# A complex recurrence rewritten as a real scan of turned drives, its matrices built on GpSimd, and the experts' last step shared between two engines

## The reference, cut to what matters

```python
act = gelu(einsum('td,ted->te', hx, expert_u[ix]))
out = einsum('te,ted->td', gx * act, expert_v[ix])
```

```python
# x_t = Lbar x_{t-1} + Bbar u_t ; y_t = Re(C x_t) + D u_t      (Lbar, Bbar, x, C complex)
lb_re, lb_im = mag * cos(li * step), mag * sin(li * step)
_, _, x_re, x_im = lax.associative_scan(_complex_combine, (a_re, a_im, bu_re, bu_im), axis=1)
y = einsum('gcp,blgp->blgc', c_re, x_re) - einsum('gcp,blgp->blgc', c_im, x_im) + d * u
```

## Time and profile before

| | us |
|---|---|
| median of 3 runs | 4241.28 |
| lowest, highest | 4234.16, 4241.31 |
| profiled execution, its own time | 4232.69 |
| profiled execution, its span | 4230.9 |

### The profile page before, as it was taken

One profiled execution on the slowest core, in us unless ns is written; L12 is line 12 of the kernel. 1 busy time (PEld: TensorE's weight loads), 2 busy tenths in 40 slices (PEclk: granted clock), 3 DMA queues, 4 the chain that ended last, 5 costly groups with the idle time before them and its releaser, 6 DMA issues. The chain is left out here.

```text
span 4230.9 us, 40117 instructions
## 1 busy us (share of the span) xinstructions
PE 3323.8 (79%) x14240; PEld 2288.4 (54%) x14240; DVE 2392.8 (57%) x3390; ACT 1209.3 (29%) x1907; POOL 898.8 (21%) x737
## 2 busy tenths in 40 slices
PE   5899995658999827777787777769996687957598
PEld 1687773437897713233233232338874476845487
DVE  1754225657975485665665665335436355577674
ACT  1422122334433401111111111024433233444652
POOL 0000004001000056455455465200002000042210
PEclk8899996778999969999999999989996598976699
DMA  9664230008953579999999999926540044500063
GB/s 361 264 254 163 89 106 17 7 6 303 368 179 124 162 305 427 427 427 427 427 428 427 428 428 427 428 103 198 192 143 11 19 150 143 174 16 5 13 198 127
DMA packets 177365, 941.68 MB, mean 223 GB/s; under 512 B 21960, under 2 KB 27336, under 8 KB 98920
## 3 DMA queue, kind: packets, MB, share of 16 engines
q0 software_dynamic: 82944, 604.02, 34.4%
q1 hardware_dynamic: 94320, 336.46, 23.2%
HBM read 938.31 MB, written 2.10 MB: 222 GB/s over the span
## 5 line engine op out<-in xcount | busy, mean ns | idle before, releaser
L1409 PE MATMUL bank<-pe_v_rows,pe_diag 128*128 128x512 f32 x2048 | 956.9, 617 | 344.3 <-DMA pe_v_rows<-in_expert_v,pe_staged_v 202.5
L1409 PEld LDWEIGHTS bank<-pe_v_rows,pe_diag 128*128 128x128 f32 x2048 | 385.6, 196 | 914.9 <-issue 594.4
L1307 DVE SCALAR_TENSOR_TENSOR pe_junk<-pe_u_rows,h_rows 128x2048 f32<-128x2048 f32 x256 | 586.9, 2293 | 443.6 <-DMA pe_u_rows<-in_expert_u,pe_staged_u 432.6
L1251 POOL DMA_INDIRECT pe_v_rows<-in_expert_v,pe_staged_v x256 | 312.0, 1219 | 367.6 <-PE bank L1409 307.3
L1251 POOL DMA_INDIRECT pe_u_rows<-in_expert_u,pe_staged_u x256 | 336.9, 1316 | 228.6 <-DVE pe_junk L1307 145.4
L1377 ACT ACTIVATE pe_diag<-ident,pe_weights 128x128 f32<-128x128 f32 x256 | 97.7, 399 | 773.3 <-PE bank L1409 768.0
L347 DVE TENSOR_TENSOR in_rest<-in_ring,in_top 128x1024 fp32r<-128x1024 f32 x112 | 136.2, 1225 | 278.5 <-ACT in_top L316 278.4
L246 PE MATMUL bank<-h_parts,b_top 128*128 128x512 f32 x768 | 274.2, 402 | 9.1 <-DVE b_rest L347 9.0
L347 DVE TENSOR_TENSOR c_rest<-c_ring,c_top 128x1024 fp32r<-128x1024 f32 x128 | 159.1, 1246 | 134.4 <-ACT c_top L316 134.4
L316 ACT ACTIVATE in_top<-in_ring 128x1024 fp32r<-128x1024 f32 x112 | 118.8, 1061 | 382.8 <-PE bank L276 193.9
L347 DVE TENSOR_TENSOR ab_rest<-ab_ring,ab_top 128x1024 fp32r<-128x1024 f32 x112 | 137.3, 1226 | 156.1 <-ACT ab_top L316 156.1
(11 more groups left out here) (479 smaller groups left out, 6464.3 us busy)
## 6 DMA issues: line engine op xcount, KB each, us to landing
b_ring<-in_w_mix SPq DMA_DIRECT2D x128, 512.0 KB, 5.8
in_ring<-in_w_in SPq DMA_DIRECT2D x112, 512.0 KB, 3.8
ab_ring<-in_w_ab SPq DMA_DIRECT2D x112, 512.0 KB, 4.2
mod_ring<-in_w_mod SPq DMA_DIRECT2D x32, 1024.0 KB, 7.9
v_rows<-in_w_mod POOLq DMA_DIRECT2D x32, 1024.0 KB, 7.0
k_cols<-in_w_mod POOLq DMA_DIRECT2D x32, 1024.0 KB, 8.1
c_ring<-in_w_c_in SPq DMA_DIRECT2D x64, 512.0 KB, 4.5
c_ring<-in_w_glu_out SPq DMA_DIRECT2D x64, 512.0 KB, 4.2
```

Source lines behind the costliest of these rows:

```text
L1251: gp.indirect_dma_start(buf[:, slot, :], None, table, bass.IndirectOffsetOnAxis(ap=staged[which][:, tile, e:e + 1], axis=0)).then_inc(sems ...
L1307: nc.vector.scalar_tensor_tensor(out=junk[:, :], in0=ub[:, s, :], scalar=1.0, in1=h2tm[:, tile, :], op0=ALU.mult, op1=ALU.mult, accum_out= ...
L1409: mm = nc.tensor.matmul(banks[4 * tile + b][:, :], diag[:, e % 4, :], vb[:, s, b * 512:(b + 1) * 512], start=False, stop=False, skip_group ...
```

## The change

Experts: the last step's rows 8 to 15 are gathered into the `u` slots, which wait only for the last dot products. Its 16 rows are divided: TensorE takes eight, VectorE multiplies and sums the other eight in `junk`. Tile 0 is copied, turned and added to `xT` meanwhile; for tile 1 VectorE adds the bank and `junk`, TensorE turns, VectorE adds. The stage that did this before is gone.

Tables: `leaps` is replaced by `turns`, unit phases for 64 groups held as 8 + 8 factors, and `decay`, the magnitude of 4 steps.

State space stage: the drives are multiplied by the opposite phase, the real and the imaginary part are each scanned by one instruction with a real multiplier, and the states are turned back. `prepare` expands the phases. The read matrices are GpSimd's too, in halves of eight pairs, from `S5Rows`; for q = 0 it makes both kinds during the stream `c_in`, whose ring has three slots for four. `kernels(q+1)` now stands in the middle of `states(q+1)` and ahead of `outputs(q)`, and writes one bank in four groups of 32 partitions; `x` and `m` have one buffer. `take_own` copies the rows of a group's own step into `now` for `kernels` (two ScalarE instructions for each q). The groups of 4 tokens lie in their natural order, so `take_u` reads and `put` writes every 4th number.

```diff
+        summed, copied, joined, turned, added = sem("po_summed"), sem("po_copied"), sem("po_joined"), sem("po_turned"), sem("po_added")
+        LAST = (N - 1) * TOPK
+        by_pe, by_dve = (0, 2, 4, 6, 8, 10, 12, 15), (1, 3, 5, 7, 9, 11, 13, 14)
+        ytm = h2tm
+        def last_row(eng, e):
+            if e < SLOTS:
+                eng.wait_ge(v_in[e], (N - 1) * 32 + 16)
+                return vb[:, e, :]
+            eng.wait_ge(u_in[e - SLOTS], N * 32 + 16)
+            return ub[:, e - SLOTS, :]
...
+                    if not u and e >= SLOTS:
+                        gp.wait_ge(u_used, LAST + e + 1)
+                        gp.sem_inc(passed, 1)
+                        gp.indirect_dma_start(ub[:, s, :], None, t["expert_v"], bass.IndirectOffsetOnAxis(ap=staged["v"][:, 1, e:e + 1], axis=0)).then_inc(u_in[s], 16)
+                        continue
...
+            def add_rows(tile, f0):
+                for f in range(f0, f0 + 8):
+                    if f % 4 == 0:
+                        dve.wait_ge(turned, 4 * tile + f // 4 + 1)
+                    part = xT[:, f, tile * P:(tile + 1) * P]
+                    nc.vector.scalar_tensor_tensor(out=part, in0=banks[4 * tile + f // 4][:, (f % 4) * P:(f % 4 + 1) * P], scalar=g2[:, f:f + 1], in1=part,
+                                                   op0=ALU.mult, op1=ALU.add).then_inc(added, 1)
+            for k, e in enumerate(by_dve):
+                row, by = last_row(dve, e), wts[:, 1, e:e + 1]
+                if k == 0:
+                    nc.vector.tensor_scalar(junk[:, :], row, by, None, ALU.mult).then_inc(summed, 1)
+                else:
+                    dve.wait_ge(summed, k)
+                    nc.vector.scalar_tensor_tensor(out=junk[:, :], in0=row, scalar=by, in1=junk[:, :], op0=ALU.mult, op1=ALU.add).then_inc(summed, 1)
+                if e in (7, 9):
+                    add_rows(0, 0 if e == 7 else 8)
+            dve.wait_ge(summed, len(by_dve))
+            dve.wait_ge(v_used, LAST + len(by_pe))
+            for b in range(4):
+                part = slice(b * 512, (b + 1) * 512)
+                nc.vector.tensor_tensor(ytm[:, 1, part], banks[4 + b][:, :], junk[:, part], ALU.add).then_inc(joined, 1)
+            add_rows(1, 0)
+            add_rows(1, 8)
+            dve.wait_ge(added, 2 * KT)
...
+            gelu(N - 2, 0)
+            diagonals(N - 2, 0)
+            gelu(N - 1, 1)
+            act.wait_ge(weights_done, N)
+            for k, e in enumerate(by_pe):
+                act.wait_ge(v_used, LAST + k - 3)
+                nc.scalar.activation(diag[:, k % 4, :], con["ident"], ACT.Copy, scale=wts[:, 1, e:e + 1]).then_inc(diag_done, 1)
+                if k == 3:
+                    for b in range(4):
+                        nc.scalar.activation(ytm[:, 0, b * 512:(b + 1) * 512], banks[b][:, :], ACT.Copy).then_inc(copied, 1)
...
+            with pe.Fori(0, E8 - 1) as i:
+                for tile in range(IT):
+                    step(i * 2 + tile, i, tile)
+            step(N - 2, E8 - 1, 0)
...
+            for k, e in enumerate(by_pe):
+                row = last_row(pe, e)
+                pe.wait_ge(diag_done, LAST + k + 1)
+                for b in range(4):
+                    mm = nc.tensor.matmul(banks[4 + b][:, :], diag[:, k % 4, :], row[:, b * 512:(b + 1) * 512], start=False, stop=False,
+                                          skip_group_check=True)
+                mm.then_inc(v_used, 1)
+                if e in (6, 8):
+                    turn(0, (0, 1) if e == 6 else (2, 3), copied)
+            turn(1, range(4), joined)
...
+            mul(decay[:, :], mag[:, :], mag[:, :])
+            mul(decay[:, :], decay[:, :], decay[:, :])
+            def square(out, a):
+                mul(z1[:, :, 0, 0:PAIRS], a, a)
+                add(out[:, 0], z1[:, 0, 0, 0:PAIRS], z1[:, 1, 0, 0:PAIRS], ALU.subtract)
+                link(nc.vector.scalar_tensor_tensor(out=out[:, 1], in0=a[:, 0], scalar=2.0, in1=a[:, 1], op0=ALU.mult, op1=ALU.mult))
+            link(nc.vector.memset(turns[:, 0, 0, :, :], 1.0))
+            link(nc.vector.memset(turns[:, 1, 0, :, :], 0.0))
+            square(double[:, 0], unit[:, :, :])
+            square(turns[:, :, 1, 0, :], double[:, 0])
+            square(double[:, 0], turns[:, :, 1, 0, :])
+            square(double[:, 1], double[:, 0])
+            square(turns[:, :, 1, 1, :], double[:, 1])
+            wheel = turns[:, :, :, :, :].rearrange("p s i f q -> p s i (f q)")
+            for a, b, n in ((1, 1, 1), (1, 2, 2), (1, 4, 3)):
+                x, by = wheel[:, :, a:a + n, :], [wheel[:, k:k + 1, b:b + 1, :].broadcast_to([P, 2, n, 2 * PAIRS]) for k in range(2)]
+                mul(z1[:, :, 0:n, :], x, by[0])
+                mul(z2[:, :, 0:n, :], x[:, ::-1], by[1])
+                add(wheel[:, 0, a + b:a + b + n, :], z1[:, 0, 0:n, :], z2[:, 0, 0:n, :], ALU.subtract)
+                add(wheel[:, 1, a + b:a + b + n, :], z1[:, 1, 0:n, :], z2[:, 1, 0:n, :])
...
+class S5Rows:
+    C = 16
...
+    def product(self, link, q, steps, table, rows, out, op):
+        nc, C = self.nc, self.C
+        p1, p2 = self.b1[:, :, 0:steps, :], self.b2[:, :, 0:steps, :]
+        for n0 in range(0, QP, QP // 2):
+            here, pairs = slice(n0, n0 + QP // 2), slice(q * QP + n0, q * QP + n0 + QP // 2)
+            for p, (k, n) in zip((p1, p2), rows):
+                row = self.raw[q % 2][:, here, k, :].unsqueeze(2).broadcast_to([P, QP // 2, steps, C])
+                by = table[:, n, :, pairs].rearrange("p s q -> p q s").unsqueeze(3).broadcast_to([P, QP // 2, steps, C])
+                link(nc.gpsimd.tensor_tensor(p, row, by, ALU.mult))
+            for part, cols in self.own_group:
+                link(nc.gpsimd.tensor_tensor(out[part, here, :, cols], p1[part], p2[part], op))
...
+    def read(self, link, q):
+        table = self.tables[1]
+        self.product(link, q, STEP + 1, table, ((2, 0), (3, 1)), self.h[q % 2][:, :, 0], ALU.subtract)
+        self.product(link, q, STEP + 1, table, ((2, 2), (3, 3)), self.h[q % 2][:, :, 1], ALU.add)
...
+            nc.gpsimd.memset(rows.h[1][:, :, :, :, :], 0.0).then_inc(cleared, 1)
+            for q in range(1, NQ):
+                gp.wait_ge(raw_in[q % 2], 16 * ((q + 1) // 2))
+                gp.wait_ge(turned, 8 * q)
+                rows.drive(link, q)
+                gp.sem_inc(gt_done, 1)
+                if q == 1:
+                    gp.wait_ge(cleared, 1)
+                else:
+                    gp.wait_ge(y_done, 2 * (q - 1))
+                rows.read(link, q)
+                gp.sem_inc(h_done, 1)
...
             def kernels(q):
...
+                if q >= 1:
+                    pe.wait_ge(h_done, q)
+                pe.wait_ge(own_done, 2 * q + 2)
                 pe.wait_ge(d_done, q + 1)
...
+                if q >= 2:
+                    pe.wait_ge(m_out, 16 * (q - 1))
+                for c in range(4):
+                    for r in range(4):
+                        out = banks[2 + q % 2][32 * r:32 * r + 32, c * P:(c + 1) * P]
                         for s in range(2):
...
+                            nc.tensor.matmul(out, now[:, 4 * c + r, s, :], rows.h[q % 2][:, 4 * c + r, s, 0:STEP, :].rearrange("p s c -> p (s c)"), start=(s == 0), stop=False)
+                        mm = nc.tensor.matmul(out, diag[32 * r:32 * r + 32, q % 2, c, :], eye[32 * r:32 * r + 32, :], start=False, stop=True)
+                mm.then_inc(within, 1)
...
+            states(0, range(4))
             kernels(0)
             for q in range(NQ):
                 if q + 1 < NQ:
                     turn(q + 1)
...
+                    states(q + 1, range(2))
+                    kernels(q + 1)
+                    states(q + 1, range(2, 4))
                 outputs(q)
...
+            def take_own(q):
+                if q >= 1:
+                    act.wait_ge(raw_in[q % 2], 16 * ((q + 1) // 2))
+                    act.wait_ge(within, q)
+                else:
+                    act.wait_ge(zeroed, 2)
+                for part, cols in rows.own_group:
+                    nc.scalar.activation(now[part, :, :, cols], rows.raw[q % 2][part, :, 0:2, :], ACT.Copy).then_inc(own_done, 1)
...
             def take_x(q):
...
+                if q >= 1:
+                    act.wait_ge(scanned, q)
                 for n in range(4):
                     act.wait_ge(driven, 4 * q + n + 1)
...
+                    src = banks[4 + n % 2][:, :].rearrange("p (q s g) -> p s q g", q=4, s=2)
+                    nc.scalar.activation(drives[:, :, 4 * n:4 * n + 4, :], src, ACT.Copy).then_inc(x_in, 1)
             def take_m(q):
...
+                act.wait_ge(zeroed, 2)
+                if q >= 1:
+                    act.wait_ge(y_done, 2 * q)
+                act.wait_ge(within, q + 1)
+                for r, s in stack:
+                    src = banks[2 + q % 2][32 * r:32 * r + 32, :].rearrange("p (q c) -> p q c", q=4)
```

(74 more changed lines are left out.)

202 lines of the change are left out of this document (67 added, 135 removed).

## The result

| | before | after |
|---|---|---|
| median of 9 runs, us | 4235.72 | 4245.21 |
| ratio, 95% interval | | 1.0022 (1.0013 to 1.0031) |
| span of the profiled execution, us | 4230.9 | 4246.4 |

The account below looks back on a forecast made before the run. TensorE bounds the experts' end, VectorE the tables; the state space stage is a loop of handings over with no full engine. -20.9 + 6.5 + 1 + 6.5 = -6.9 from 4241.3 gives 4234.4 us, range 4198 to 4262.

Parts of the forecast that it names:

- What bounds: Whole kernel: TensorE sets the experts' end, VectorE works alone in tables, the state space stage has no full engine.
- Experts, -20.9: Experts' last step: rows shared by TensorE and VectorE bring the norm 20.9 us earlier; bounds 18.5 to 22.7.
- 2771.2 + 3.45 + 0.3: Experts' end: last gather landed, then TensorE's row of 3.45 us at full clock, through at 2775.0.
- Tables, +6.5: Tables' stage: 5.8 us of old work gone, 12.3 us new, all on the path; bounds +5 to +8.
- c_in, +1: Stream c_in: GpSimd's 32 instructions for q = 0 go under it, costing 1 us; bounds 0 to +5.
- State space, +6.5: State space stage: 307.2 us for 300.7, start 15 us shorter, kernels(1) late, cycle longer; bounds -40 to +35.
- `outputs(0)` at 1.00, 10.7: State space stage, first cycle: outputs(0) behind half of states(1) runs at full clock in 10.7 us, to 126.5.
- rival A: State space stage: GpSimd later than ScalarE at kernels(2) and kernels(3), TensorE idles, clock low: 4255 to 4275; chance 0.19.
- B: State space stage: the clock holds or rises at once at kernels(1), -10.7 and -3.5, 4220 us; chance 0.12.
- C: State space stage: ScalarE's copies at every 4th number are cheap: 4228 us, 4220 to 4245; chance 0.12.
- D: State space stage: kernels' four groups of 32 output partitions run beside each other: 4200 to 4210 us; chance 0.14.
- E: Experts' end isn't shortened, since gathers or VectorE's last row land late: 4242 to 4255 us; chance 0.07.

Follow-up runs that it names:

- 170 needless turns: Changed kernel with 170 needless TensorE turns during the wait for h(1) and 126 ahead of outputs(3): ratio 0.9956, stage 296.2 us.
- the runs with early h(1): Changed kernel with read matrices of q = 1 to 3 on VectorE: ratio 0.9937; also with row 15 on VectorE and TensorE's and ScalarE's orders changed: 0.984.
- the last run: Changed kernel with read matrices and row 15 on VectorE, kernels(q+1) behind outputs(q), put(q) ahead of take_m(q+1), 62 needless turns ahead of outputs(3): 0.9815, 4160.0 us.

## Why the prediction was wrong

- **What bounds.** Right: a loop of handings over with no full engine. That VectorE's shorter recurrence brings nothing in this order was right as well: in the changed kernel's trace no wait of TensorE or ScalarE within the stage ends with VectorE. In another order, with the read matrices on VectorE, the stage takes 248 us where it took 301 before the change.
- **Experts, -20.9.** -18.5 in the changed kernel, -19.5 alone. The step at fault is "2771.2 + 3.45 + 0.3": the last row was costed at the full clock. TensorE, now sharing the rows, had waited 3.66 us for it and took 6.43. Counted from the last dot product, that row also started 1 us later than I had it. With VectorE doing that row it is -22.7. Of the prices behind it, joins and additions took 2.48 and 4.21 us for my 2.75 and 5.3.
- **Tables, +6.5.** Right: 3475.53 to 3487.92 is 12.4 us for 12.3.
- **c_in, +1.** +1.3 in the pair of traces; this stage varies from 183.3 to 187.8 over the runs, so no more than the bounds can be told.
- **State space, +6.5; measured +23.3.** The steps one by one: kernels(0) at 25.5 (24.5 forecast), h(1) at 86.7 (84), kernels(1) at 0.50 for 24.9 us (24.7), half of states 7.1 (7.1). Then came the step that failed: "`outputs(0)` at 1.00, 10.7". It took 20.7, at 0.50. I had let the half of `states(1)` raise the clock, as the turns had at 3785; the rows from 3800 to 3846, which I quoted under rival A, said otherwise. That is 10 of the 17 us, and that it is the clock is shown by the 170 needless turns, with which outputs(0) took 10.9. h(1) is 2.7: GpSimd's 32 products started 1.1 later than forecast and were stretched by some 24 us, not 20, by VectorE's instructions between them (`prepare` took 11.4 us undisturbed, priced at 8.0), while on their own they would have been 2 shorter than priced. From outputs(0) to kernels(2) it is 2.0, of which 1.3 is the load of ScalarE's gelu table ahead of `put(0)`: the price of 13.05 was that of a later `put`, which has no such load. The later cycle was 71.3 us for 69.8, and the rest, under 1, lies in the end.
- **Rival A** gave the right sign but too much (4255 to 4275, measured 4245), and by another mechanism: kernels(2) and kernels(3) waited for ScalarE as forecast and ran at 1.00; what ran low was outputs(0), in the first cycle. **B** is refuted in the changed kernel, and is what the long idle work brings about (stage -28). **C** is refuted: 657 and 389 ns. What the Trainium skill says in "SBUF — State Buffer" in its note on 16-byte cachelines, that one can stride for free up to 4 fp32 numbers, did not hold for these copies: 4 numbers cost what 32 do. **D** is refuted: kernels(2) took 14.2 us at 1.00, with four groups of 32 partitions in turn, as with one before. The parallel work that the Trainium skill's "TensorEngine Tiling (Array Packing)", Key Properties, tells of can't be seen in it. Of the drain at a change of mode, which the same section tells of, the pair of kernels shows nothing: both change between 128x32 and 32x32 tiles for every pair of channel groups. **E** did not come about: the experts' end was shortened by 18.5 us.

## What to carry to other kernels

Lay out the first cycle of a pipelined stage apart from the steady one, with the clock of each piece: here 41 us lay in one wait (17) and the low clock behind it (24), more than the 18.5 that the change had gained in the experts. Ask of a moved job not only how long it takes on the new engine but what it is queued behind there and whose instructions it alternates with. When an engine's work becomes much shorter and nothing is gained, look at the order in which its neighbours hand over: here the swap of `put` and `take_m` and the place of `kernels` together, with the read matrices on VectorE, took the stage to 248 us. That the shorter scan made this possible is argued and not shown: VectorE was busy 230 us of the stage before, which would leave 248 little room, but no run has the old scan in the new order.

## What the hardware showed that was not expected

TensorE stayed at 0.50 through 52 us of gapless kernels, states and outputs (3791 to 3843), though at each of the other turns in the traces of both kernels some 3 to 7 us of gapless turns and states raised it (kernels(2) ran at 1.00). Once at 1.00, it stayed there through the same kernels and outputs (25 us in the runs with early h(1)).

It was lost in 8.0 us of idle time behind needless turns, around the 3.7 us ahead of the experts' last row, and around the 2.7 us ahead of outputs(0) in the kernel before. It was not lost across the 0.5 us between the needless turns and outputs(3) in the last run. In the run with 126 turns it fell in the second half of outputs(3), behind a wait of 0.4 us and one of 1.0 us; the last run has no second wait there. Whether that makes the difference stays open, since the experts' rows ran at 1.00 across waits of 1.2 us each.
